# One decoder step on one core: the SSD scan cut into small items between the projection tiles, x projected first

## The reference, cut to what matters

```python
hn = rmsnorm(h, norm_mix); proj = hn @ w_in          # z, xbc, dt, q, k, v
y_ssd, new_conv, new_ssm = ssd_branch(z, xbc, dt, ...) # conv, scan in chunks of 128, gate by silu(z), rmsnorm
y_att = moba_attention(q, k_all, v_all, ...)          # 8 heads; sample: 1024 past tokens from pages
h = h + concat[y_ssd, y_att] @ w_out
h = h + cross_attend(rmsnorm(h), mk, mv, w_q, w_o)    # 4 heads over 256 memory tokens
h = h + square(relu(rmsnorm(h) @ w_up)) @ w_down
```

## Time and profile before

| | before |
|---|---|
| median of 3 runs | 818.47 us (818.47 to 819.72) |
| the profiled execution, its span | 817.9 us |
| PE busy | 736.1 us, 90% |
| LDWEIGHTS busy | 517.9 us, 63% |
| DVE busy | 286.2 us, 35% |
| ACT busy | 137.8 us, 17% |
| POOL busy | 71.0 us, 9% |
| moved by DMA | 125.94 MB, 154 GB/s on average |

### The profile page before, as it was taken

The page is one execution under the profiler, slowest core; times in us unless marked ns, Lnnn a source line. Parts: engine busy times, 40 slices in busy tenths (PEclk is TensorE's granted clock), DMA queues, the critical chain, the costliest instruction groups (busy, mean ns, idle before and its releaser), DMA issues. The chain is left out here.

```text
span 817.9 us, 10472 instructions
## 1 busy us (share of the span) xinstructions
PE 736.1 (90%) x3583; PEld 517.9 (63%) x3583; DVE 286.2 (35%) x625; ACT 137.8 (17%) x302; POOL 71.0 (9%) x136
## 2 busy tenths in 40 slices
PE   4779999997999998879699978699999999999993
PEld 2456777775665665433257755467777777777772
DVE  2252254255757614972782324432111110000003
ACT  2132133131111304321110004211111110000002
POOL 3020001021010004000241100020000000000000
PEclk9969999998999997979799989999999999999997
DMA  9454668877688648000039802664344342623601
GB/s 282 133 163 143 217 210 267 255 227 222 199 265 272 205 107 261 1 1 0 1 100 286 292 17 104 206 175 133 116 140 151 111 148 78 205 101 104 205 0 59
DMA packets 102475, 125.94 MB, mean 154 GB/s; under 512 B 6385, under 2 KB 78565, under 8 KB 102440
## 3 DMA queue, kind: packets, MB, share of 16 engines
q1 hardware_dynamic: 99240, 115.08, 45.0%
q0 software_dynamic: 3200, 10.39, 4.5%
HBM read 117.14 MB, written 8.31 MB: 153 GB/s over the span
## 5 line engine op out<-in xcount | busy, mean ns | idle before, releaser
L820 PE MATMUL ps<-hw,wring 128*128 128x288 f32 x576 | 151.8, 425 | 5.7 <-DVE qs L1618 3.7
L820 PEld LDWEIGHTS ps<-hw,wring 128*128 128x128 f32 x576 | 114.3, 200 | 42.1 <-DVE qs L1618 4.1
L1235 PE MATMUL ps<-big,wring 128*128 128x288 f32 x512 | 124.4, 406 | 1.5 <-ACT big L1531 1.5
L1221 PE MATMUL ps<-hw,wring 128*128 128x288 f32 x512 | 124.3, 406 | 0.0
L1235 PEld LDWEIGHTS ps<-big,wring 128*128 128x128 f32 x512 | 97.2, 190 | 28.7 <-issue 2.0
L1221 PEld LDWEIGHTS ps<-hw,wring 128*128 128x128 f32 x512 | 97.3, 190 | 26.9
L1380 ACT ACTIVATE tmp<-ps 128x512 f32<-128x512 f32 (+4 forms) x71 | 39.7, 562 | 255.4 <-PE ps L1063 130.1
L1572 DVE COPY tmp<-ps 128x512 f32<-128x512 f32 (+3 forms) x84 | 53.6, 643 | 68.4 <-PE ps L806 62.4
L806 PEld LDWEIGHTS ps<-ident,big 128*128 128x128 f32 x400 | 46.5, 148 | 38.3 <-issue 13.4
L806 PE MATMUL ps<-ident,big 128*128 128x128 f32 x400 | 59.6, 293 | 11.5 <-DVE tmp L1572 6.3
L1985 DVE SCALAR_TENSOR_TENSOR big<-ps,rstd 128x288 f32 x32 | 14.6, 457 | 105.8 <-PE ps L1221 105.5
(11 more groups left out here) (258 smaller groups left out, 656.0 us busy)
## 6 DMA issues: line engine op xcount, KB each, us to landing
wring<-in_w_in SPq DMA_DIRECT2D x16, 1024.0 KB, 6.8
big<-in_cache_k SPq DMA_DIRECT2D x64, 256.0 KB, 2.7
big<-in_cache_v SPq DMA_DIRECT2D x64, 256.0 KB, 3.6
wring<-in_w_up SPq DMA_DIRECT2D x16, 1024.0 KB, 5.4
wring<-in_w_down SPq DMA_DIRECT2D x16, 1024.0 KB, 4.9
wring<-in_w_out SPq DMA_DIRECT2D x8, 768.0 KB, 8.7
wring<-in_w_ca_kv SPq DMA_DIRECT2D x4, 1024.0 KB, 5.2
big<-in_state_ssm SPq DMA_DIRECT2D x8, 512.0 KB, 5.8
```

Source lines behind the costliest of these rows:

```text
L820: last = pe.matmul(ps[:, t % 2, 0:width], w, rhs(c * k_tiles + k), start=(c + k == 0), stop=(c == chunks - 1 and k == k_tiles - 1))
L1221: last = pe.matmul(ps[:, t % 2, 0:T], wring[:, s, k * 256 + half * P:k * 256 + half * P + P], hw[:, k, :], start=(k == 0), stop=(k == DT - 1))
L1235: last = pe.matmul(ps[:, t % 2, 0:T], wring[:, s, k * 256 + half * P:k * 256 + half * P + P], ff[:, c * T:(c + 1) * T], start=(c == 0), st ...
```

## The change

- Every projection is given tile by tile, and the scan as entries of `SEQ` of their own: `tok`, `sums`, `seg`, `yo`, `sst`, `stt`, `upd`, `yd`, `ys`, `zsq`, `state`.
- x is projected first, then dt and z, then q/k and v. The sample chunk of the scan comes first (`CHUNKS = [2, 0, 1]`), among the z and q/k tiles; chunk 0 among the v tiles; chunk 1 among K units with no projection tile between them. The K units start after the first v tiles.
- The memory input is loaded and transposed after the scan (`memt`); `m` tiles and the first part of the output projection (`oz`, the SSD rows) lie among V units and self heads; the second part (`oa`, the attention rows) follows.
- All PSUM results of the scan go through the turns; a turn has a fixed engine where the result is used directly. Prompt head scores (`hs`) go through the turns too. Several copies fall away (`mix` works in place, the gate and the y results read PSUM). The meeting of all engines before the scan goes; after it stands `over`, where ACT and DVE wait for each other.
- Weight blocks are asked for when the block four before is used up, units when the unit two before is.

The plan, from the scan on:

```diff
-    pair("qk", 0, 1)
-    item("ss", 0)
-    item("early")
...
+    pair("x", 0)
+    item("hist")
+    item("ss", "x")
+    for n in range(1, 6):
+        pair("x", n)
+    unit("ST", 0)
+    unit("ST", 1)
+    item("dt")
+    tile("z", 0, 0)
+    item("dt_series")
+    tile("z", 0, 1)
+    item("dt_rates")
+    tile("z", 1, 0)
+    item("silu_x")
+    tile("z", 1, 1)
+    tile("z", 2, 0)
+    item("cv")
+    tile("z", 2, 1)
+    tile("z", 3, 0)
+    item("tok", 2)
+    tile("z", 3, 1)
+    item("silu_z")
+    item("sums", 2)
+    tile("qk", 0, 0)
+    item("seg", 2, 0)
+    item("stt", 0, 4)
+    tile("qk", 0, 1)
+    item("stt", 4, 10)
+    tile("qk", 1, 0)
+    item("stt", 10, 16)
+    tile("qk", 1, 1)
+    item("yd")
+    item("upd", 0, 2)
+    tile("qk", 2, 0)
+    item("upd", 2, 5)
+    item("ys")
+    tile("qk", 2, 1)
+    item("upd", 5, 8)
+    tile("qk", 3, 0)
+    item("upd", 8, 11)
+    tile("qk", 3, 1)
+    item("upd", 11, 14)
+    item("tok", 0)
+    tile("v", 0, 0)
+    item("upd", 14, 16)
+    item("sums", 0)
+    tile("v", 0, 1)
+    item("seg", 0, 0)
+    unit("K", 0, 0)
...
+    tile("v", 1, 0)
...
+    tile("v", 1, 1)
+    item("seg", 0, 3)
+    item("yo", 0, 2)
+    unit("K", 0, 1)
+    item("yo", 0, 3)
+    item("sst", 0)
+    item("kvtok")
+    item("tok", 1)
+    item("sums", 1)
     unit("K", 0, 2)
+    item("seg", 1, 0)
+    item("seg", 1, 1)
     unit("K", 0, 3)
+    item("yo", 1, 0)
+    item("seg", 1, 2)
     item("own", 0)
+    item("yo", 1, 1)
+    item("seg", 1, 3)
     unit("K", 1, 0)
+    item("zsq", 0)
+    item("yo", 1, 2)
+    item("zsq", 1)
+    item("yo", 1, 3)
+    item("sst", 1)
     unit("K", 1, 1)
+    item("zsq", 2)
+    item("zsq", 3)
+    item("state")
+    item("over")
+    item("heads_in", "self")
+    unit("K", 1, 2)
+    item("ss", "ssd")
     item("probs", 0)
+    item("head", "self", 0)
+    item("memt")
     unit("K", 1, 3)
     item("own", 1)
+    item("head", "self", 1)
+    item("ss", "mem")
+    pair("m", 0)
+    unit("V", 0, 0)
+    item("head", "self", 2)
...
+    pair("m", 3)
     item("mtok")
     unit("V", 0, 3)
     item("pvend", 0)
+    item("head", "self", 5)
     item("probs", 1)
+    pair("oz", 0)
     unit("V", 1, 0)
...
+    pair("oz", 3)
     for n in range(4):
-        pair("out", n, 2)
+        pair("oa", n)
```

The waits and the gate of the prompt heads, the stores of the states and the loads:

```diff
+            def store_states(h):
+                src = kvring[:, UNIT[("ST", h)] % 2].rearrange("p b a (c n) -> p b (a c) n", n=SN)
+                turned(pool, ("up", 8 * h + 7))
+                for b in range(GB):
+                    store(O["sample_ssm"][h * GB + b].rearrange("(c p) n -> p c n", p=P), src[:, b], st_out[h])
...
                 elif s == ("heads_in", "self"):
-                    in_ps(pool, ("mvtok", 1))
+                    pool.wait_ge(ssd_over, 2)
+                    in_ps(pool, ("sf", 1))
                     pool.wait_ge(rb_out, 16)
                     load_bias(0), load_bias(1)
...
+                elif s == ("tok", 0):
+                    load_unit(2)
+                elif s == ("seg", 0, 0):
+                    load_unit(3)
+                elif s[0] == "unit" and s[1] != "ST" and UNIT[s[1:]] + 2 < len(UNITS):
+                    load_unit(UNIT[s[1:]] + 2)
+                elif s[0] == "over":
+                    sp.wait_ge(ssd_over, 2)
+                    sp.wait_ge(turn_ps, TURN[("sf", 1)] + 1)
+                    sp.dma_start(memin, I["mem_prompt"].rearrange("(g p) n -> p g n", p=P)).then_inc(mem_in, 16)
...
-                    dve.wait_ge(bias_in[x % 2], 32 * (x // 2 + 1))
-                    step(dve.scalar_tensor_tensor(PL[:, x % 2], sc, DH ** -0.5, biasP[:, x % 2, :, ::-1],
-                                                  ALU.mult, ALU.add))
+                    key = ("hs", x)
+                    in_ps(dve, key)
+                    sc = ps[:, bank(key), :].rearrange("p (q k) -> p q k", q=2)
+                    dve.wait_ge(bias_in[x % 2], 32 * (x // 2 + 1))
+                    dve.scalar_tensor_tensor(PL[:, x % 2], sc, DH ** -0.5, biasP[:, x % 2, :, ::-1],
+                                             ALU.mult, ALU.add).then_inc(turn_dve, 1)
```

More of the change, by code:

```diff
@@ L122, in make_plan, with pair, tile @@
     seq = []
-    def pair(kind, n, chunks):
-        seq.append(("pair", kind, n, chunks))
+    def pair(kind, n):
+        seq.append(("tile", kind, n, 0))
+        seq.append(("tile", kind, n, 1))
+    def tile(kind, n, half):
+        seq.append(("tile", kind, n, half))
     def unit(*a):
@@ L271, in plan_turns @@
         elif s[0] == "own":
-            turn(("own", s[1]))
+            turn(s)
         elif s[0] == "probs":
@@ L361, in build @@
         attT = sb("attT", [P, 4, T])
+        vT = attT
         mkv = sb("mkv", [P, 2048])
@@ L832, in out_tile @@
                     pe.wait_ge(heads_out, 2)
[L833 to L845 removed]
+                if kind == "cao" and first:
+                    for x in range(CROSS):
+                        turned(pe, ("pv", "cross", x))
+                    pe.wait_ge(scores_used, 4)
+                    pe.wait_ge(heads_out, 4)
@@ new lines, in tile @@
+                for k in range(K_TILES[kind]):
+                    if first and kind == "x":
+                        pe.wait_ge(hw_done, k + 1)
+                    elif first and kind == "caq":
+                        pe.wait_ge(hw_done, 8 + k + 1)
+                    elif first and kind == "m":
+                        pe.wait_ge(memw_done, k + 1)
+                    elif first and kind == "oz":
+                        pe.wait_ge(z_scaled, k + 1)
+                    if kind == "m":
+                        rhs, width = memw[:, k, :], NP_
+                    elif kind == "oz":
+                        rhs, width = z[:, k, :], T
+                    elif kind in ("oa", "cao"):
+                        rhs, width = attT[:, k, :], T
+                    else:
+                        rhs, width = hw[:, k, :], T
+                    w = wring[:, slot, k * 256 + half * P:k * 256 + half * P + P]
+                    last = pe.matmul(ps[:, t % 2, 0:width], w, rhs, start=(k == 0), stop=(k == K_TILES[kind] - 1))
@@ L1138, in _ @@
             for s in SEQ:
-                if s[0] == "pair":
-                    pair(*s[1:])
-                elif s[0] == "early":
+                if s[0] == "tile":
+                    tile(*s[1:])
+                elif s[0] == "hist":
+                    pe.wait_ge(cv_in, 16)
+                    transposes("conv", [(cvin[:, c * P:(c + 1) * P], c * 24) for c in range(XT)])
+                elif s[0] == "memt":
                     pe.wait_ge(mem_in, 16)
@@ L1468, in _ @@
+            leave("vec")
+            for c in range(DT):
+                leave(("x", c))
+                turned(act, ("x", c))
+                square("x", c, h3[:, c, :], T)
             for s in SEQ:
@@ new lines, in gate @@
+            def gate(q, hg):
+                off, n = TOKS[q]
+                key = ("y", q, hg)
+                in_ps(dve, key)
+                if q == 0 and hg == 0:
+                    dve.wait_ge(z_silu, 1)
+                for j in range(2):
+                    c = 2 * hg + j
+                    last = dve.scalar_tensor_tensor(ybuf[:, hg % 2, j * P:(j + 1) * P], xc[:, c, off:off + n],
+                                                    dec[:, c, NB:NB + 1], ps[:, bank(key), j * P:(j + 1) * P],
+                                                    ALU.mult, ALU.add)
+                last.then_inc(turn_dve, 1)
+                turned(dve, key)
+                zz = z[:, 2 * hg:2 * hg + 2, off:off + n]
+                dve.tensor_tensor(zz, zz, heads(ybuf[:, hg % 2, :], 2, P), ALU.mult).then_inc(y_used, 1)
@@ new lines, in sample_gate @@
+            def sample_gate():
+                n = NS
+                in_ps(dve, "ys")
+                dve.wait_ge(z_silu, 1)
+                for c in range(DT):
+                    last = dve.scalar_tensor_tensor(ybuf[:, 0, c * n:(c + 1) * n], xc[:, c, NP_:T], dec[:, c, NB:NB + 1],
+                                                    ps[:, bank("ys"), c * n:(c + 1) * n], ALU.mult, ALU.add)
+                last.then_inc(turn_dve, 1)
+                turned(dve, "ys")
+                dve.tensor_tensor(z[:, :, NP_:T], z[:, :, NP_:T], heads(ybuf[:, 0, :], DT, n), ALU.mult)
```

1260 lines of the change are left out of this document (599 added, 661 removed).

## The result

| | before | changed |
|---|---|---|
| median | 818.47 us | 851.83 us (848.95 to 853.40, 4 runs) |
| the profiled execution, its span | 817.9 us | 851.3 us |
| PE busy | 736.1 us, 90% | 739.9 us, 87% |
| DVE busy | 286.2 us | 286.4 us |
| clock | 0.953 | 0.946 |

The changed kernel is slower: ratio 1.0424, interval 1.0381 to 1.0467. The forecast was 840 within 795 to 860, with 0.60 for slower.

The account below looks back on a forecast made before the run. PE bounds the kernel, waiting mostly in the scan, where cutting could give at most 33 us; stages of PE work, waits and 6 us of clock reach 489.5, plus 350.7 unchanged gives 840.2 us, range 795 to 860.

Parts of the forecast that it names:

- from the final states over the bias rows to the K unit behind: K stretch: PE waits 17 us at state, over and heads_in, including final states 4 and bias rows 9.3.
- own 0: K stretch: 6.8 us of waits around it, as DVE's choice of blocks holds up ACT and then PE.
- store of k and start of chunk 1: K stretch: 5.6 us of waits at the end of chunk 0, kvtok and the start of chunk 1.
- keys: Before the first K unit: its load waits for the state stores, taken as 5 us of stall.
- own 1: Among memory tiles and V units: 5.5 us of waits for own 1 and the memory norm together.
- segments and y of chunk 0: K stretch: 6.6 us of waits around two v tiles.
- K stretch: First to last K unit, with chunks 0 and 1: 95 us of PE work plus 43 of waits, from 214 to 352.
- four long stalls: Stalls of 5.6 to 17 us slow the clock afterwards: 1.5 us each, 6 in all.
- rival C: K stretch runs at clock 0.87 like the old scan stretch, costing 14 us: about 852, chance .10.
- Rival B: K loads arrive late, six units by 1.5 us each, and stores before the first two cost 5: 854, chance .08.
- Rival A: From 214 us on, listed waits of 61.5 us stay under 39.5 because PE's three-turn lead suffices: about 803, chance .34.
- q/k stretch: q/k tiles with the sample chunk: 90 us or less as the sign, over 100 would speak against the forecast.

Follow-up runs that it names:

- e1: Changed kernel with the prompt heads' bias rows given memory free after the last v tile, so their loads issue earlier: 842.85 us, ratio 1.0359.
- e7: Changed kernel with only own 1 moved behind the first memory tile pair: 847.98 us, ratio 1.0400.
- e4: Changed kernel with a third slot for staging k, so copying the sample rows need not wait for a store: 844.45 us, ratio 1.0394.
- e8: Changed kernel with six moves together: early bias rows, last v pair, second K unit, third staging slot, joined norms, own 1: 824.97 us, ratio 1.0128.
- e2b: Changed kernel with the last v tile pair moved right behind own 0 and kvtok to just before the fifth K unit: 851.79 us, ratio 1.0457.
- e5: Changed kernel with only the second K unit moved behind the sums of chunk 1: 849.61 us, ratio 1.0389.
- e9: e8 with the prompt's final state moved ahead of the last squares and the third K unit behind two segments of chunk 1: 819.13 us, ratio 1.0036.

## Why the prediction was right, and where it was not

- **The sign and its reason are right.** The loss is made where K units have no projection tile beside them. Most waits named came up where they were put: from the final states over the bias rows to the K unit behind 14.9 (17 expected), of it 5.5 for the states (4), 7.2 for the bias rows and 2.2 in short ones behind; own 0 5.6 (6.8), store of k and start of chunk 1 4.0 (5.6), keys 3.5 (5 before the first K unit, where only gaps under 1 came), own 1 4.1 and the bias rows of head 7 6.5 (5.5 and 6). One did not come: segments and y of chunk 0 have 1.1 of waits for 6.6. The norm of the scan result with the memory transposes has 7.6 for 5. So the 39.7 of waits against 43 is in part luck: errors of 2 to 6 us either way cancel. Run e1 shows the largest of them as a cause, e7 that of own 1, e4 that of the store.
- **The stages.** Forecast 214 for the start of the K units, measured 217.7: 1.7 of it before the first tile, 1.2 in the norm. K stretch forecast 138, measured 151.1. From its end to `oa` 121 with the clock term, measured 117.3. `oa` 16.5 and 15.5. Rest 350.7 and 349.7.
- **The step that was mis-sized is the clock.** I took 1.5 us for each of four long stalls, 6 in all. In the K stretch alone it is 17.8, beside 39.7 of waits (43 in the sum) and 93.6 of work (95). Of the 11 us by which the span exceeds the sum, this term is about the whole; the other differences cancel. The price of rival C, 14, was nearer, and its time of 852 fits the 851.3: it and the forecast's waits both came, though the fit has luck in it, 4 too little for the clock and 3 too much for the waits. The Trainium skill (TensorE: Matmul & The Clock Gate, "A second HAM failure mode: psum-queue depth-cycling") describes, for another kernel in bf16, a clock that goes down where short idles part the groups, and the trace agrees in kind with 0.84. That the clock costs those 17.8 by itself no run isolates: it goes with the waits (from the sums of chunk 0 to the first memory tile 17.0 in the changed kernel, 13.0 in e1, 11.6 in e8), and the one run that kept PE busy in two gaps gained nothing.
- **Rival B** was given too little for the place and too much for the size. Keys were late once, by 3.5, in the changed kernel, and by 2.3 in its second profile. But they stood close behind: e2b and e5 turned gaps elsewhere into 9.84 and 3.83 of key waits. **Rival A** asked for under 39.5 of the listed waits; e9 shows that the design can come within 0.4% of the kernel before, with 22.8 of idle time left from the sums of chunk 0 to the first memory tile, but only with eight further changes.
- **The q/k stretch** with the states and updates took 92.5, idle 2.9: over the 90 named as its sign, under the 100 that would have spoken against it.
- **Signs.** The K stretch gave them (151.1 us, clock 0.84, a DVE wait of 9.59 for the bias rows, ACT waiting 6.02 for DVE ahead of own 0), but for one: behind the head scores PE was to be idle for over 10, and had 9.1.
- **Two readings in the forecast are off,** and the sum uses neither. Ahead of 312.7 lie not 9.3 us of PE's work but 6.27 (a V unit and pieces of heads; the z tiles end at 303.2), so the most that the scan stretch could give was (94.78 - 6.27) x 0.87 = 77 of work, 107 - 77 = 30, not 33. And of the first pair only the first eight products are slow, .69 each, the later ones .41.

## What to carry to other kernels

Cutting a latency-bound part into items worked here where every cut lay beside work with buffers of its own (2.9 us idle of 131.7), and not where none did (39.7 of 151.1); count how many such tiles are left for the last chunk before laying the first. Here x first and the states' hold on both key slots pushed the K units behind all projection tiles but two. Loads that hang on the end of a phase (bias rows, keys behind stores) are due at the very place that the cutting has made bare: give them memory that is free earlier. And where PE's work is parted by short gaps, price the clock from the stretch that already looks like it, not from single stalls.

## What was not expected of the hardware

- The same instructions can get another clock. From `caq` (the first product behind `oa`) to the end the changed kernel and all runs made from it do the same work; e1 and e8 have the same 32.8 us of idle time in it, and it took 349.9 us in e1 and 354.3 in e8:

```profile
489.90:839.80 349.90, 317.08 (x1401) 241.97 (x1399) 56.06 (x118) 42.25 (x95) 9.98 (x21) 0.97 0.37 118
```

```profile
467.90:822.20 354.30, 321.55 (x1401) 244.60 (x1399) 56.06 (x118) 42.25 (x95) 10.01 (x21) 0.96 0.36 116
```

All of the 4.4 us is PE's busy time, 321.55 against 317.08, at a clock of 0.96 against 0.97. It lies in three short places of 1.6 to 1.7 us each, less 0.4 in the pair before them. One of them came and went between two profiles of the changed kernel itself, in the MLP's first loop:

```profile
584.53 124.32 PE L1300 MATMUL ps<-hw,wring 128*128 128x288 f32 x512
```

```profile
581.20 126.01 PE L1300 MATMUL ps<-hw,wring 128*128 128x288 f32 x512
```

So a part of it belongs to the single execution and not to the kernel. Some of what the profiles of e8 and e9 lack to the kernel before (350.70 there) is this. It is not shown what decides it.
- PE kept busy with products through two long gaps did not have full clock behind three gaps of 1.3 to 2.2 us.
